# Two prompt steps for one sample step, from the value pages on, in the sparse stage of a two-layer decoder

## What is computed

```python
h = x + W_out [ SB(xn) | RET(xn) | NSA(xn) ]      # xn = RMSNorm(x)
y = h + W_down relu(RMSNorm(h) W_up)^2
# NSA, for each query block of the prompt:
o_c, o_s = nsa_cmp_slc(qb, pb, kcmp, vcmp, ks_blk, vs_blk)   # compressed blocks, selected blocks
o_w = window_attn(qb, kwb, vwb, pb, kpos)                    # sliding window
o_nsa3 = stack([o_c, o_s, o_w])                              # then mixed by sigmoid gates
# the sample side reads the caches through a page table:
rows = cache[l][page_table]                                  # sb_k, sb_v, cmp_k, cmp_v, slc_k, slc_v
```

## Time and profile before

| What | us |
|---|---|
| three runs | 2004.73, 1996.4, 2004.06; median 2004.06 |
| the profiled execution, whole | 2000.34 |
| its span (first to last instruction) | 1998.6 |
| PE busy in the span | 1812.7 (91%) |
| sparse stage, first layer, from the scores of unit 17 to its end | 459.75 to 545.20 |
| the same, second layer | 1439.43 to 1526.30 |

### The profile page before, as it was taken

How to read it: one execution, slowest core, us unless ns; L and a number is a source line. 1 busy time by engine, 2 the same in 40 slices (tenths; PEclk the granted TensorE clock), 3 DMA queues, 4 the chain that set the end, 5 groups by cost and what they waited for, 6 DMA issues and landing times. The chain is left out here.

```text
span 1998.6 us, 25485 instructions
## 1 busy us (share of the span) xinstructions
PE 1812.7 (91%) x9442; PEld 1442.3 (72%) x9442; DVE 886.7 (44%) x1749; ACT 519.5 (26%) x1313; POOL 534.5 (27%) x718
## 2 busy tenths in 40 slices
PE   6999887778799999999999998787878999999998
PEld 5888664444487888888878886644545788888887
DVE  4035336875354444443320642468543544343433
ACT  2122323344522211111111224244444222020202
POOL 0006102846032221212300330057350312221222
PEclk7999888788699999999999998778786999999999
DMA  6411403547412222222242204045390222222223
GB/s 204 169 43 43 118 11 108 182 156 262 118 43 85 85 85 85 85 85 85 85 153 80 85 1 128 2 160 210 120 318 15 85 83 86 85 85 85 85 85 127
DMA packets 107931, 210.35 MB, mean 105 GB/s; under 512 B 28128, under 2 KB 37136, under 8 KB 103328
## 3 DMA queue, kind: packets, MB, share of 16 engines
q1 hardware_dynamic: 92944, 141.58, 21.4%
q0 software_dynamic: 13824, 67.12, 9.2%
q10 hardware_dynamic: 1040, 0.00, 0.0%
HBM read 200.00 MB, written 17.06 MB: 109 GB/s over the span
## 5 line engine op out<-in xcount | busy, mean ns | idle before, releaser
L527 PE MATMUL ps<-xt,ring 128*128 128x260 f32 x1536 | 349.5, 387 | 8.8 <-DVE xt L663 8.8
L527 PEld LDWEIGHTS ps<-xt,ring 128*128 128x128 f32 x1536 | 291.9, 193 | 54.6 <-issue 9.9
L2120 ACT ACTIVATE tt<-ps 128x260 f32<-128x260 f32 x108 | 41.8, 387 | 355.0 <-PE ps L2019 236.2
L2120 ACT ACTIVATE scr<-ps 128x260 f32<-128x260 f32 x108 | 41.8, 387 | 352.4 <-PE ps L2019 229.0
L1218 PE MATMUL ps<-cst,xt 128*128 128x128 f32 x328 | 75.5, 343 | 46.8 <-ACT xt L1281 35.7
L1218 PEld LDWEIGHTS ps<-cst,xt 128*128 128x128 f32 x328 | 43.8, 171 | 90.5 <-ACT xt L1281 62.4
L605 ACT ACTIVATE tt<-ps 128x520 f32<-128x520 f32 x48 | 28.9, 602 | 289.9 <-PE ps L527 289.9
L1359 DVE TENSOR_REDUCE small<-ps 128x1 f32<-128x512 f32 (+3 forms) x128 | 56.8, 485 | 96.3 <-PE ps L1203 96.1
L1827 POOL TENSOR_TENSOR tt<-ring,tt 128x1024 f32<-128x1024 f32 x32 | 82.6, 2594 | 45.1 <-DVE scr L1630 32.3
L2065 POOL TENSOR_TENSOR x_fm<-x_fm,scr 128x260 f32<-128x260 f32 x60 | 50.7, 844 | 160.8 <-DVE scr L2275 54.3
L1955 PE MATMUL ps<-big,ring 128*128 128x260 f32 x384 | 92.3, 382 | 0.0
(11 more groups left out here) (418 smaller groups left out, 3716.6 us busy)
## 6 DMA issues: line engine op xcount, KB each, us to landing
ring<-in_w_up SPq DMA_DIRECT2D x16, 2048.0 KB, 8.3
ring<-in_w_down SPq DMA_DIRECT2D x16, 2048.0 KB, 7.9
ring<-in_w_in SPq DMA_DIRECT2D x15, 2048.0 KB, 8.0
ring<-in_state_win_k SPq DMA_DIRECT2D x2, 2048.0 KB, 8.4
ring<-in_state_win_v SPq DMA_DIRECT2D x2, 2048.0 KB, 14.2
ring<-in_w_out SPq DMA_DIRECT2D x4, 1024.0 KB, 13.5
ring<-in_w_out SPq DMA_DIRECT2D x8, 512.0 KB, 16.9
out_s_win_k<-in_state_win_k SPq DMA_DIRECT2D x2, 2044.0 KB
```

The lines of the kernel that those rows point to most:

```text
L527: ins = pe.matmul(self.ps[:, 2 * (u % 2) + half, 0:H], w[:, k, f * P:(f + 1) * P], self.xtv[:, k, half * H:(half + 1) * H], start=(k == 0) ...
L2120: act.activation(tmp(u, j), bank(u, 0), ACT.Copy).then_inc(done, 1)
```

## The change

From sample step 34 on, which is the first half of value page 0, every engine's program takes two steps of the prompt, then one of the sample. Before that step nothing moves. No instruction is added or taken away on any engine.

```diff
+VALUES_FROM = 34
...
         def in_turn(eng, name):
             a, b = prompt[name](eng), sample[name](eng)
-            live = [a, b]
+            step, live = 0, [a, b]
             while live:
-                for g in list(live):
-                    if next(g, live) is live:
+                turn = [a, b] if step < VALUES_FROM else [a, a, b]
+                step += 1
+                for g in turn:
+                    if g in live and next(g, live) is live:
                         live.remove(g)
```

## The result

The changed kernel takes 1977.76 us (median of 4 runs, 1976.16 to 1978.96) where the kernel before took 2004.39 in runs beside it: a ratio of 0.9866, with a 95% interval of 0.9826 to 0.9907. The forecast was 1979.0, with 1960 to 2000 around it. The profiled execution has a span of 1974.4 us, against 1998.6, and a mean granted clock of 0.937, against 0.922.

What follows compares the result with a forecast made beforehand. Idle PE and time at 1.2 GHz bound the stretch: 56.4 us work plus 13 waits, taken as 69, plus 0.25 x 27, gives 75.7 a layer; saving 21 from 2000.34 gives 1979 us, range 1960 to 2000.

Steps and rivals of the forecast that it cites:

- What bounds the stretch: Unit 17's scores to stage end: 18.9 and 18.3 us without a product, plus 36% and 46% at 1.2 GHz.
- the idle time has two places: PE idles in that stretch at waits for page sums, and from unit 27 in a PE, DVE, ACT chain without pages.
- PE's work: PE's products from unit 17's scores to stage end: about 56.4 us a layer at full clock, against 85.45 taken.
- the first rival: DVE's sums cost nothing, tail stays at 2.4 GHz: stretch 62 to 66 us a layer, 1952 to 1966; chance 0.10.
- Waits that stay: PE waits left from unit 17's scores to stage end: 13 us a layer, giving 69 us at full clock.
- tail: The five last turns keep the chain's wait, 0.64 us each, with the end about 4 us.
- The terms for sum and copy: Page sums before gates, 3 us in all; two compressed value products waiting for ACT's copy, 3.4 us.
- The clock: A quarter of the stretch at 1.2 GHz: 17% for the last turns, 8% for copy waits and what follows.
- POOL's round: Gathers of pages 3 to 7 wait for PE, hidden while a pair (6.8 us or more) outlasts POOL's 6.0 us.
- w_out: Its loads start at about 503 instead of 491.68 and land before the stage ends: no cost, up to 5 us.
- POOL against DVE: Rival: DVE's gates meet POOL's multiplication once a page, pages 2 to 7: 24 us, 2003, no gain; chance 0.10.
- What would show me wrong: Stretch clock below 0.7, L1347 often over 1 us, page sum waiting over 5 us for POOL, or `mix_and_mlp` awaiting w_out.

Runs made afterwards that it cites:

- the turn from 44: Changed kernel with the two-to-one turn starting at sample step 44 instead of 34: 1979.18 us, ratio 0.9889 to the kernel before.
- the early copy: Changed kernel with ACT copying a tile's finished output ahead of that unit's exponentials: 1962.95 us, ratio 0.9817 to the kernel before.
- the order with the sum between gate and maxima: Changed kernel with DVE's page sum between one unit's gate and the next unit's maxima: 2007.26 us, ratio 1.0027 to the kernel before.
- the kernel from 28 with the early copy: Changed kernel with the turn from step 28 and a tile's output copied ahead of ACT's exponentials: 1948.17 us, ratio 0.9736 to the kernel before.

## Why the prediction was right

- **What bounds the stretch.** Right for the pages, and shown: with PE's waits for them gone and the collision at unit 18 left (the turn from 44) the ratio is 0.9889, with the change 0.9866. That idle time costs about as much again by the clock was right too: 11.9 us of idle time and 11.2 of busy time went with the change, 6.9 and 4.9 with the early copy. But "the idle time has two places" missed a third, the 2.61 us at unit 18, and "PE without gaps" in units 17 and 18 ends right ahead of it.
- **PE's work.** 56.4 us at the full clock, and 6.75 for a quarter of the time at the lower level, make 63.1; 61.99 and 61.90 were measured. In the first rival, 62 to 66 us a layer give 1952 to 1960, not 1966; no chance rests on it.
- **Waits that stay.** The total was right by luck: tail 1.2 instead of 4, page 7 nothing instead of 1, the wait with the collision at unit 27 3.78 instead of nothing. Luck, too, that this new wait is near the 2.61 that went at unit 18, as neither was counted. The terms for sum and copy were right to 0.1 us, since they came from the order on DVE and ACT and from rows.
- **The clock.** The size was right (22% for 25%), the place wrong: I carried the low end of the earlier trace rows over to the new end. Most of the low level comes behind PE's longest waits (3.78 and 1.77), and these now stand at the first units of tile 0.
- **POOL's round.** Right: the pair (7.2 us) is longer than the round (6.0), so gathers that wait for PE cost nothing. Page 7 at 1 us was safe.
- **w_out.** "No cost" was right, but it was more than that: out of page 7's way it is worth 10 us in the order before.
- **POOL against DVE.** Given a tenth, and half seen. That before "DVE mostly waits for that multiplication and issues nothing beside it" was wrong once a layer: L1339 took 3.05 us. The reason against the rival, that the gate is usually ahead of the multiplication, holds for L1347 in the changed kernel, by 0.04 us; the compressed unit's gate, which has more instructions behind the sum, was not looked at. That the rival was real is shown by the order with the sum between gate and maxima: 2007.
- **What would show me wrong.** Clock 0.89, not under 0.7; no sum that waits for POOL; `mix_and_mlp` doesn't wait for w_out; L1347 at 0.16 in the stretch. None came. The scores' starts were 2.7 and 4.5 us apart in tile 1, a mean of 3.6, in the 3 to 4 named; in tile 0 the first two were 8.7 and 5.7 apart (496.42, 505.08, 510.77), against 2.5 to 3, and then 2.4 to 3.0.

## What to carry to other kernels

When two streams share engines in a fixed order, first find which steps of the slower stream are really late: here three of eight pages, and giving just these a second partner brought most of the gain. Then try other starts of the turn: here the best of four was the one where the slow stream ends with the other, but each start also makes or avoids collisions, so the trace of each has to be read. When an instruction takes ten times its usual length, look for it in the kernel before as well: an experiment that shortens the other engine's work removes that loss too. And before an idle engine is filled, follow what would release the moved step: if the same event starts work on another engine that shuts the first one out, the two meet every time, as they did in every page here.

## What the hardware showed that I had not expected

- A VectorE instruction of 8 elements a partition, with one tensor in SBUF and a per-partition scalar, was held beside a POOL multiplication as one with two tensors is: 2046 and 2049 ns beside it, 0.23 us away from it. The gate, a tensor_tensor of 2 elements a partition, took up to 2.60 us in the stretch of the kernel with the moved sum, and L1339, of 128 elements, 3.05 before the change.
- That L1339 had started 0.54 us ahead of the multiplication (469.40 and 469.94), while POOL issued a gather, and was held all the same; the instruction ahead of it took 0.17 beside the same issue. What held it in that half microsecond was not tested.
- Behind a wait of 3.79 us the clock was 0.50 from 1466.50 to 1473.20 with PE busy all the time (second layer, early copy); in the changed kernel, with a second wait of 1.51 at 1480.49, it was 0.50 from 1472.00 to 1485.40. In the kernel from 28 with the early copy, whose waits in tile 1 are 0.41 at most, the clock is 1.00 from 461.86 to 491.00.
- A transfer of 1024 KB took 5.5 us instead of 13.5 to land (medians) when its loads started 13 us later, past the gathers, and 8.5 where all of w_out was issued at once behind the last page.
